# A hybrid DeltaNet and attention encoder: query and key tiles with their heads interleaved row by row, and tile stores issued from ScalarE's queue

## What is computed

```python
h = _rmsnorm(x, norm_w[l])
proj = jnp.einsum('btd,dc->btc', h, w_in[l])
dn_qkv, dn_z, dn_b, dn_a, at_q, at_k, at_v, at_z = jnp.split(proj, splits, axis=-1)
...
q = _axial_rope(_rmsnorm(q, q_norm_w), row, col)      # 8 heads of 64
k = _axial_rope(_rmsnorm(k, k_norm_w), row, col)      # 2 heads of 64
o = _block_attention(q, k, v)
```

## Time and profile before

| | |
|---|---|
| three runs, median (lowest to highest) | 4551.25 us (4546.82 to 4556.17) |
| the profiled execution, its own time | 4553.01 us |
| its span, first to last instruction | 4551.2 us |
| TensorE busy | 3938.0 us, 87% |
| VectorE busy | 2696.9 us, 59% |
| ScalarE busy | 1856.8 us, 41% |
| granted TensorE clock, mean | 0.936 |
| the main DMA queue, share of 16 engines | 29.4% |

### The profile page before, as it was taken

One profiled execution on the slowest core, in us unless ns is written; L12 is line 12 of the kernel. 1 busy time (PEld: TensorE's weight loads), 2 busy tenths in 40 slices (PEclk: granted clock), 3 DMA queues, 4 the chain that ended last, 5 costly groups with the idle time before them and its releaser, 6 DMA issues. The chain is left out here.

```text
span 4551.2 us, 57469 instructions
## 1 busy us (share of the span) xinstructions
PE 3938.0 (87%) x19701; PEld 3070.6 (67%) x19701; DVE 2696.9 (59%) x3334; ACT 1856.8 (41%) x2590; POOL 671.2 (15%) x760
## 2 busy tenths in 40 slices
PE   3999994679989999987889999746997999999694
PEld 2788883569856666655758888634996666666473
DVE  5543043557778888874255402426676888888432
ACT  3321110335457777761132211012554777777310
POOL 0011100387500000000000110015952000000000
PEclk9999997789989999998989999868998999999896
DMA  6111143545520000016231112445454000000635
GB/s 242 63 70 69 56 139 139 150 108 144 136 65 24 23 22 23 23 67 185 107 128 70 55 69 92 149 128 124 134 159 113 23 21 23 23 23 17 168 134 209
DMA packets 335159, 423.02 MB, mean 93 GB/s; under 512 B 104408, under 2 KB 254024, under 8 KB 312208
## 3 DMA queue, kind: packets, MB, share of 16 engines
q1 hardware_dynamic: 333840, 412.49, 29.4%
q10 hardware_dynamic: 1152, 8.39, 0.5%
HBM read 272.89 MB, written 147.91 MB: 92 GB/s over the span
## 5 line engine op out<-in xcount | busy, mean ns | idle before, releaser
L1732 DVE TENSOR_REDUCE att_sb_part<-att_banks 128x1 f32<-128x512 f32 x992 | 658.9, 685 | 151.7 <-PE att_banks L1617 144.3
L1720 ACT ACTIVATE att_sb_probs<-att_banks 128x1024 f32<-128x1024 f32 x512 | 525.4, 1026 | 379.2 <-PE att_banks L1643 379.0
L1750 DVE TENSOR_TENSOR att_sb_p_lo<-att_sb_probs,att_sb_p_hi 128x1024 fp32r<-128x1024 f32 x512 | 623.6, 1218 | 22.6 <-ACT att_sb_p_hi L1724 20.5
L348 PE MATMUL proj_banks<-proj_sb_h_hi,proj_sb_w_hi 128*128 128x512 f32 x1600 | 523.5, 408 | 76.0 <-DVE proj_sb_w_lo L482 76.0
L1724 ACT ACTIVATE att_sb_p_hi<-att_sb_probs 128x1024 fp32r<-128x1024 f32 x512 | 543.6, 1062 | 16.2
L348 PE MATMUL proj_banks<-proj_sb_h_lo,proj_sb_w_hi 128*128 128x512 f32 x1600 | 518.9, 406 | 0.0
L348 PE MATMUL proj_banks<-proj_sb_h_hi,proj_sb_w_lo 128*128 128x512 f32 x1600 | 518.4, 405 | 0.0
L1041 PE MATMUL dn_banks<-dn_sb_room 128*128 128x128 f32 x3072 | 380.5, 284 | 57.5 <-DMA dn_sb_room<-proj 27.4
L1041 PEld LDWEIGHTS dn_banks<-dn_sb_room 128*128 128x128 f32 x3072 | 369.0, 199 | 80.0 <-DMA dn_sb_room<-proj 37.3
L1659 PE MATMUL att_banks<-att_sb_p_hi,att_sb_v_hi 128*65 128x512 f32 x1024 | 406.4, 397 | 12.6 <-DVE att_sb_o L1756 11.2
L1642 PE MATMUL att_banks<-att_sb_q,att_sb_k 128*128 128x512 f32 x1024 | 413.8, 404 | 1.9 <-DVE att_sb_q L1744 1.9
(11 more groups left out here) (226 smaller groups left out, 5618.8 us busy)
## 6 DMA issues: line engine op xcount, KB each, us to landing
proj<-proj_sb_out SPq DMA_DIRECT2D x52, 1024.0 KB, 4.6
dn_sb_kq<-proj SPq DMA_DIRECT2D x64, 512.0 KB, 5.4
proj_sb_w_raw<-in_w_in SPq DMA_DIRECT2D x52, 516.0 KB, 5.2
dn_sb_room<-proj SPq DMA_DIRECT2D x32, 768.0 KB, 5.3
att_sb_q<-att_q SPq DMA_DIRECT2D x64, 256.0 KB, 2.8
out_sb_x<-x_res SPq DMA_DIRECT2D x16, 1024.0 KB, 6.6
x_res<-out_sb_x SPq DMA_DIRECT2D x16, 1024.0 KB, 4.2
out_sb_w_raw<-in_w_out SPq DMA_DIRECT2D x24, 512.0 KB, 5.2
```

Source lines behind the costliest of these rows:

```text
L348: mm = nc.tensor.matmul(ps[:, 2 * half + n, :], w[:, u, k, :], h[:, k, at:at + QB], start=(k == 0 and w is w_hi and h is h_hi), stop=(k == ...
L1720: nc.scalar.activation(probs[:, pair % 2], ps[:, 2 * (pair % 2):2 * (pair % 2) + 2, :], ACT.Exp, scale=SCALE).then_inc(s["exp_done"], 1)
L1732: nc.vector.tensor_reduce(part[:, w // NQ, w % NQ:w % NQ + 1], ps[:, 4 + w % 2, :], AX.X, ALU.max) \
L1750: nc.vector.tensor_tensor(p_lo[:, pair % SLOTS], probs[:, pair % 2], p_hi[:, pair % SLOTS].bitcast(F32), ALU.subtract).then_inc(s["lo_done ...
```

## The change

Three things.

1. The channels of the query and key tiles are permuted, on the host, so that partition p holds row p // 4 of head p % 4. A key tile's row group of four is key head 0, key head 1, and two value channels. The tables, norm weights and the indicator for the sums follow the same order. A key unit now works on 128 partitions (with the value rows computed and not stored), and `qk_rows` has 12 rows instead of 10.
2. With this order the stores of a query unit have 32 rows outermost and the 4 heads inside, and the load of the inverse norms has 32 outermost too. A key unit has eight stores of 32 partitions (every fourth) x 512 instead of four of 64 x 512. The values are picked out of the key tiles by a strided load.
3. The stores of tiles 20 to 25 leave SP's order and are issued by ACT, right after its evacuations. Tile 19's store stays with SP, ahead of the loop.

```diff
-N_ROWS = ATT_HEADS + KV_HEADS
+PAIR_HEADS = 4
+N_ROWS = PAIR_HEADS * PAIR_TILES
...
-                    sp.dma_start(ab[u][0:parts], a.proj[T_AQ + 2 * pair:T_AQ + 2 * pair + 2, 0:parts, cols]
+                    sp.dma_start(ab[u], a.proj[T_AQ + 2 * pair:T_AQ + 2 * pair + 2, :, cols]
                                  .rearrange("f p t -> p f t")).then_inc(s[f"ab_loaded{u}"], 16)
-                    heads = parts // QUARTER
-                    sp.dma_start(inv[u][0:parts], a.qk_rows[4 * pair:4 * pair + heads, cols].unsqueeze(1)
-                                 .broadcast_to([heads, QUARTER, QB])).then_inc(s[f"inv_loaded{u}"], 16)
+                    sp.dma_start(inv[u], a.qk_rows[PAIR_HEADS * pair:PAIR_HEADS * (pair + 1), cols].unsqueeze(0)
+                                 .broadcast_to([QUARTER, PAIR_HEADS, QB])).then_inc(s[f"inv_loaded{u}"], 16)
...
                     for src, low in ((yy[u], 0), (xx[u], DH)):
                         sp.wait_ge(s["lo" if low else "hi"], n + 1)
                         for half in range(2):
-                            row = low + half * QUARTER
-                            sp.dma_start(dst[:, row:row + QUARTER, at:at + QB], src[0:parts, half, :]) \
-                                .then_inc(s[f"rope_stored{u}"], 16)
+                            rows = slice(low + half * QUARTER, low + (half + 1) * QUARTER)
+                            if pair < PAIR_TILES - 1:
+                                dst = a.att_q[PAIR_HEADS * pair:PAIR_HEADS * (pair + 1), rows, cols]
+                                sp.dma_start(dst.rearrange("h r t -> r h t"), src[:, half, :]) \
+                                    .then_inc(s[f"rope_stored{u}"], 16)
+                            else:
+                                for kv in range(KV_HEADS):
+                                    sp.dma_start(a.att_k[kv, rows, cols], src[kv:P:PAIR_HEADS, half, :]) \
+                                        .then_inc(s[f"rope_stored{u}"], 16)
...
                 load_unit(1)
+                store_tile(ROPE_TILE - 1)
                 for t in range(ROPE_TILE, N_TILES):
                     load_weights(t)
-                    store_tile(t - 1)
...
-                store_tile(N_TILES - 1)
...
                 for t in range(ROPE_TILE, N_TILES):
                     plain(t // 2, t % 2, ACT.Silu, t + 1 < N_TILES)
+                    act.dma_start(a.proj[t], out[:, t % 2, :]).then_inc(s[f"out_stored{t % 2}"], 16)
...
-                    sp.dma_start(v[kv * DH:(kv + 1) * DH], a.proj[T_AK + kv, DH:P]).then_inc(s["v_loaded"], 16)
+                    sp.dma_start(v[kv * DH:(kv + 1) * DH], a.proj[T_AK + kv].rearrange("(r c) t -> r c t", c=PAIR_HEADS)[:, KV_HEADS:]) \
+                        .then_inc(s["v_loaded"], 16)
...
-            parts += [at_q + h * DH + np.array(dims) for h in range(head, head + 4)]
+            parts.append(np.array([at_q + h * DH + d for d in dims for h in range(head, head + PAIR_HEADS)]))
```

More of the change, by code:

```diff
@@ L60, in rope_unit, with unit_stores @@
     pair, quarter = n % PAIR_TILES, n // PAIR_TILES
-    return pair, quarter * QB, P if pair < PAIR_TILES - 1 else P // 2
+    return pair, quarter * QB
+def unit_stores(n):
+    return sum(16 * (8 if rope_unit(m)[0] == PAIR_TILES - 1 else 4) for m in range(n % 2, n + 1, 2))
 W_BA = 2 * ITEMS
@@ L257, in load_unit @@
                         return
-                    pair, at, parts = rope_unit(n)
+                    pair, at = rope_unit(n)
                     u = n % 2
@@ L276, in store_unit @@
                 def store_unit(n):
[L277 to L280, removed]
+                    pair, at = rope_unit(n)
+                    u, cols = n % 2, slice(at, at + QB)
                     for src, low in ((yy[u], 0), (xx[u], DH)):
@@ L306, in _ @@
                         load_unit(n + 2)
-                store_tile(N_TILES - 1)
                 for u in range(2):
-                    sp.wait_ge(s[f"rope_stored{u}"], 64 * (ROPE_UNITS // 2))
+                    sp.wait_ge(s[f"rope_stored{u}"], unit_stores(ROPE_UNITS - 2 + u))
                 for u in range(2):
@@ L549, in rope_products @@
                 def rope_products(n):
-                    pair, _, parts = rope_unit(n)
+                    pair = rope_unit(n)[0]
                     u, k = n % 2, int(pair == PAIR_TILES - 1)
@@ L555, in rope_products @@
                     if n >= 2:
-                        dve.wait_ge(s[f"rope_stored{u}"], 64 * (n // 2))
+                        dve.wait_ge(s[f"rope_stored{u}"], unit_stores(n - 2))
                     for dst, half, src, weight, table in ((xx, 0, 0, w_first, 0), (yy, 0, 1, w_negative, 1),
                                                            (xx, 1, 1, w_second, 0), (yy, 1, 0, w_first, 1)):
-                        op = nc.vector.scalar_tensor_tensor(out=dst[u][0:parts, half, :], in0=ab[u][0:parts, src, :],
-                                                            scalar=qk_w[0:parts, weight:weight + 1],
-                                                            in1=rope[0:parts, table, :], op0=ALU.mult, op1=ALU.mult)
+                        op = nc.vector.scalar_tensor_tensor(out=dst[u][:, half, :], in0=ab[u][:, src, :],
+                                                            scalar=qk_w[:, weight:weight + 1],
+                                                            in1=rope[:, table, :], op0=ALU.mult, op1=ALU.mult)
                     op.then_inc(s["products"], 1)
                 def rope_rest(n):
-                    parts, u = rope_unit(n)[2], n % 2
-                    x, y = xx[u][0:parts], yy[u][0:parts]
+                    u = n % 2
+                    x, y = xx[u], yy[u]
                     dve.wait_ge(s["products"], n + 1)
@@ L570, in rope_rest @@
                     dve.wait_ge(s[f"inv_loaded{u}"], 16 * (n // 2 + 1))
-                    factor = inv[u][0:parts].unsqueeze(1).broadcast_to([parts, 2, QB])
+                    factor = inv[u].unsqueeze(1).broadcast_to([P, 2, QB])
                     nc.vector.tensor_tensor(x, x, factor, ALU.mult).then_inc(s["scaled"], 1)
@@ L2048, in constants @@
     ind = np.zeros((P, 4), f)
-    ind[i, i // QUARTER] = 1
+    ind[i, i % PAIR_HEADS] = 1
     half = DH // 2
@@ L2054, in constants @@
     for p in range(P):
-        d = FIRST_DIMS[p % QUARTER]
+        d = FIRST_DIMS[p // PAIR_HEADS]
         pos = (tok // DH if d < half else tok % DH).astype(f)
@@ L2127, in lay_out @@
     parts = []
-    for head in range(0, ATT_HEADS, 4):
+    at_k = at_q + ATT_HEADS * DH
+    for head in range(0, ATT_HEADS, PAIR_HEADS):
         for dims in (FIRST_DIMS, SECOND_DIMS):
-            parts += [at_q + h * DH + np.array(dims) for h in range(head, head + 4)]
-    at_k = at_q + ATT_HEADS * DH
+            parts.append(np.array([at_q + h * DH + d for d in dims for h in range(head, head + PAIR_HEADS)]))
     for kv, dims in enumerate((FIRST_DIMS, SECOND_DIMS)):
-        parts += [at_k + h * DH + np.array(dims) for h in range(KV_HEADS)]
-        parts.append(at_v + kv * DH + np.arange(DH))
+        parts.append(np.array([[at_k + d, at_k + DH + d, at_v + kv * DH + 2 * r, at_v + kv * DH + 2 * r + 1]
+                               for r, d in enumerate(dims)]).reshape(P))
     order = np.concatenate([np.arange(2 * conv, 3 * conv), np.arange(0, 2 * conv), *parts,
@@ L2149, in lay_out @@
     for v in (np.asarray(q_norm_w), np.asarray(k_norm_w)):
-        first, second = np.tile(v[:, FIRST_DIMS], (1, 4)), np.tile(v[:, SECOND_DIMS], (1, 4))
+        first, second = np.repeat(v[:, FIRST_DIMS], PAIR_HEADS, axis=1), np.repeat(v[:, SECOND_DIMS], PAIR_HEADS, axis=1)
         norm_cols += [first, second]
```

## The result

| | before | changed |
|---|---|---|
| median, first comparison | 4553.05 us (4 runs) | 4428.55 us (4 runs, 4427.05 to 4429.47) |
| ratio, 95% interval | | 0.9728 (0.9711 to 0.9745) |
| median, second comparison (run e7) | 4552.98 us (15 runs) | 4437.03 us (5 runs, 4430.37 to 4442.97) |
| ratio, 95% interval | | 0.9743 (0.9728 to 0.9758) |
| span of the profiled execution | 4551.2 us | 4427.6 us; second 4435.5 us |

The change is 2.7% faster in the first comparison and 2.6% in the second. The forecast was 4440 us, with a range of 4427 to 4473; the first median lies 1.6 us inside its lower edge.

The account below looks back on a forecast made before the run. DMA, its query and key stores on 4 and 2 engines, was taken to hold DVE and so PE. PE's 80.0 us plus 31.8 at the stage's end, 111.8 us, gave 4440 us; range 4427 to 4473.

Parts of the forecast that it names:

- What bounds the stage: Projection's last tiles: DMA on 4 or 2 engines holds DVE, DVE holds PE, which waits 34.9 us.
- The choice of 16 engines between the bounds of 10.6 and 2.7 us: Query unit's stores: new pattern taken to run on 16 engines, 2.7 us per unit instead of 10.6 on 4.
- SP's issues all below 1 us: Sign that the forecast is right: each DMA issue on SP in the changed kernel takes under 1 us.
- DVE's chain: Layer 1 units at 7.15 us each: split for tile 24 done at 670.7 us, 17.7 us before PE needs it.
- PE's gain: Tiles 23 to 25: waits and lower clock go, saving 39.6 and 40.4 us in the layers, 80.0 us together.
- The tile stores on ACT: Six DMA issues per layer on ACT, 0.4 us each, covered by about 10 us idle before each evacuation.
- The end of the stage: Last evacuation to next stage's first DMA: 8.6 us instead of 24.1 and 24.9, saving 31.8 us.
- The sum: Whole kernel: 80.0 + 31.8 = 111.8 us saved, giving 4440 us.
- Late units: Rival, chance 0.10: units still come late to tile 24, PE loses 28 us over two layers, 4468 us.
- the new pattern doesn't spread: Rival, chance 0.05: DMA stays the bound, only the stage's end gains 0 to 6 us per layer, about 4546 us.
- slow writing over heads 1 MiB apart: Rival, chance 0.03: query stores slow in DRAM; at 20 us per query unit the kernel takes 4605 us.

Follow-up runs that it names:

- e7: The changed kernel itself, unaltered, measured and profiled once more: 4437.03 us, ratio 0.9743 to the kernel before.
- e3: Changed kernel with each query store cut in two, 31 rows and 1 row by 4 heads: 4934.83 us in one run.
- e12: Kernel before with only the loads of the inverse norms split by head: 4504.24 us, ratio 0.9894 to before.
- e10: Kernel before with two units beside each of the last six tiles instead of 2, 3, 3, 2, 2, 0: 4551.71 us, ratio 1.0000.
- e1: Changed kernel with the tile stores back in SP's order: 4428.84 us, ratio 0.9737 to the kernel before.
- e2: Kernel before with the last six tiles' stores issued by ACT, layout unchanged: 4548.74 us, ratio 0.9998 to before.
- e5: Changed kernel with each query store cut into 25 rows and 7 rows by 4 heads: 4451.74 us, ratio 0.9793 to the kernel before.
- e4: Kernel before with tile stores on ACT and all unit stores and inverse-norm loads split by head: 4442.27 us, ratio 0.9760 to before.

## Why the prediction was right

**What bounds the stage.** The steps were DMA holds DVE, DVE holds PE, and 4 and 2 engines hold DMA. e3 shows the last by its size, one engine at 26 GB/s and 40.7 us per unit for 41 computed, and e12 shows that the chain of DMA work is the bound, 47.1 us for 46 when only the norm loads were spread. That DVE holds PE is so in the waits, but e10 shows that this link by itself did not set the time.

**The choice of 16 engines between the bounds of 10.6 and 2.7 us** was right: share 1.02 at 375 GB/s for queries, and bursts at 0.95 and 369 GB/s for keys. A key unit's eight stores take SP 4.9 us to issue, where 3.7 were reckoned from other small stores. The sign "SP's issues all below 1 us" held for most, but not for all: a load and a norm load took 1.38 and 1.28 us, and one query store 1.41.

**DVE's chain.** The split for tile 24 was forecast to be done at 670.7 us. It starts at 676.24 and is done at 677.5, 6.8 us later. The changed kernel's projection runs 2.3 us later here (668.21 for 665.91), so the chain was 4.5 us longer than worked out. Before this split the table left 3.0 us of waiting (all at unit 6, none at unit 3) where I had 1, and unit 4 waited 1.9 for its data, where I had nothing; the other 2.5 us of waiting for the table come behind the split. The table's landing was taken as near 5. The changed trace has 5.7 in the median and 3.8 to 7.4 in all, and for unit 6 DVE starts 7.5 us after the issue (654.45 to 661.92). PE needed the split at 690.7, so 13 us were spare, where 17.7 had been forecast, and none of the loss reached PE.

**PE's gain.** Forecast 39.6 and 40.4 us; three tiles took 67.46 and 67.47 instead of 107.1 and 107.9, so the gain is the same two numbers within 0.1.

**The tile stores on ACT** were costed at nothing, and the issue takes 0.34 us. What I didn't work out is that they are also worth nothing (e1 4428.84, e2 0.9998). The 29.4 us that ACT waited for an old store were a symptom of the full queue: in e2 they are gone and the time stays. This changed no number, since the gain at the end was priced with the units done.

**The end of the stage.** Forecast 8.6 us, measured 6.9: 1.1 us from evacuation to issue, and 5.8 for the landing (4.4 in the median) and the meeting of the engines, which is thus nearer 1.4 than my 3. That is 17.2 + 18.0 = 35.2 us instead of 31.8.

**The sum.** The two places give 80.0 + 35.2 = 115.2 us. The layers run 1.9 and 0.7 us longer than before up to tile 22's second evacuation, which leaves 112.6, and the two stages are 112.7 us shorter in the first profile (54.9 + 57.7) and 113.4 in the second. The forecast had 111.8. The profiled spans differ by 123.6 us, so 10.9 of them lie outside the stages: that part takes 3066.6 us in the first profile after and 3077.6 in the one before, but 3075.2 when the changed kernel is profiled again. In the other runs it lies between 3069.0 and 3073.8, with either layout, so no part of these 10.9 us is shown to be from the change. The second comparison gives 116 us (4552.98 - 4437.03). So the first measurement's distance from the forecast, 11.5 us, fits the variation between runs and no step of the sum; it took the measurement almost to the edge of the range.

**One thing the sum's form hid.** I added PE's waits and the end of the stage as two gains. e10 shows that they are one: shift the units and the first turns into the second at no change in time (PE's waits 34.9 to 1.7 us, the wait at the end 23.1 to 54.2). The sum was right because both went, with the DMA work that had been behind them. Someone who had removed only PE's waits, by that reckoning, would have forecast 80 us and got none.

**The rivals.** Late units came true in e5, where 8.9 us of PE's waiting and a stage 10 us longer fit them, though mostly at tile 25; in the change 13 us were left at tile 24. That the new pattern doesn't spread is refuted by the share, and slow writing over heads 1 MiB apart by 375 GB/s. By the Trainium skill's rule on pitches, which the prediction cites (DMA: Bandwidth & Descriptors, "Latency and other measured facts"), the estimate was 6.4 us per unit. This case shows no such loss with pieces of 2 KB at 1 MiB; larger pitches weren't tried.

## What to carry to other kernels

When a stretch waits for DMA, look at the share of the engines in a window of 2 us over one kind of transfer. A share of 0.25 or 0.13 with GB/s to match can mean that its outermost dimension spreads it over 4 or 2 engines, and splitting or reordering that dimension is then the repair, with or without a new layout. Windows of 0.1 us confirm it: there the share stays low all the time, while small stores that wait for their issue show bursts on all engines with nothing between them. Before pricing a wait that will go, ask which chain sets the end of the stage: a wait inside it that only shares the time out gives nothing back (e10), while work taken off the chain counts nearly in full (e12). A queue of its own for a transfer behind the chain gained nothing here, neither while the chain was long (e2) nor once it was short (e1).

## What was new about the hardware

- Stores of 2 KB pieces move 51 GB/s on 2 engines, 99 on 4 and 26 on one, so 25 to 26 GB/s per engine, and on all 16 the rates are 375 (query stores) and 395 (table, weights and tile store). e5's stores, of 25 and 7 rows in turn, move only 101 to 127 GB/s at shares of 0.36 to 0.40, which is 17 to 20 per busy engine. Why is open.
- 31 rows outermost cost some fifteen times what 32 cost in transfer time (40.7 us for a unit's 1 MiB in e3, with its single rows apart, against about 2.7 by the rate).
- SP is held by few-engine transfers as if it did them itself: four issues with 512 KiB in all took 20.59 us in e3, on one engine; in the change, on 16, the same bytes in two issues take 1.28 us. All that stands behind them in SP's order is then late.
- A piece of 32 x 512 takes SP about 0.46 us to issue where the partitions are contiguous (e4) and 0.60 us where they are every fourth (2.40 us for four key stores in the change). Nothing else was tried that would show why.
